# Six modulation units and a shorter routing chain between the output projection and the experts, gate applied at the bank

## The reference, cut to what matters

```python
mod = jax.nn.silu(c) @ w_ada[layer] + b_ada[layer]            # 6 x 1024 columns per layer
sh1, sc1, g1, sh2, sc2, g2 = jnp.split(mod[:, None, :], 6, axis=-1)
hcur = rms_norm(x, norm1_g[layer]) * (1 + sc1) + sh1
...                                                          # layer 0: attention and gMLP, layer 1: conv and stick-breaking
x = x + g1 * mix
hcur = rms_norm(x, norm2_g[layer]) * (1 + sc2) + sh2
x = x + g2 * hierarchical_moe(hcur, ...)
# hierarchical_moe: logits of 4 groups and 4x4 experts; best group, its two best experts
gates = jnp.sum(jax.nn.one_hot(flat_idx, N_EXPERTS) * (g_w * e_w)[..., None], axis=1)
for e in range(N_EXPERTS):                                   # 16 experts, 3 x 2 MB of weights each
    hid = jax.nn.silu(xt @ w_gate[e]) * (xt @ w_up[e])
    y = y + gates[:, e:e + 1] * (hid @ w_down[e])
```

## Time and profile before

| | us |
|---|---|
| median of 3 runs (lowest, highest) | 1408.23 (1408.17, 1416.61) |
| profiled execution, its own time | 1416.04 |
| its span | 1414.4 |
| TensorE busy | 1241.1 (88%) |
| VectorE, ScalarE busy | 355.9, 293.0 |
| mean DMA rate over the span | 248 GB/s |

### The profile page before, as it was taken

One profiled execution on the slowest core, in us unless ns is written; L12 is line 12 of the kernel. 1 busy time (PEld: TensorE's weight loads), 2 busy tenths in 40 slices (PEclk: granted clock), 3 DMA queues, 4 the chain that ended last, 5 costly groups with the idle time before them and its releaser, 6 DMA issues.

```text
span 1414.4 us, 17421 instructions
## 1 busy us (share of the span) xinstructions
PE 1241.1 (88%) x7188; PEld 728.6 (52%) x7191; DVE 355.9 (25%) x1017; ACT 293.0 (21%) x582; POOL 73.4 (5%) x126
## 2 busy tenths in 40 slices
PE   4899995898999969997958799999499999999996
PEld 1656543433334347754434333333286878767772
DVE  0212414211111122852052011111321144333212
ACT  2213302111111121134021111111300345552101
POOL 3000001000000040000000000000000123300000
PEclk8899996999999979999959899999799999999998
DMA  9995972599999997865326899999933433433000
GB/s 344 325 342 200 347 286 62 190 393 395 395 396 394 394 322 282 299 252 178 119 75 251 300 388 395 396 396 394 332 119 133 160 108 124 139 130 130 0 16 30
DMA packets 159061, 351.19 MB, mean 248 GB/s; under 512 B 4852, under 2 KB 7068, under 8 KB 159004
## 3 DMA queue, kind: packets, MB, share of 16 engines
q1 hardware_dynamic: 152776, 340.94, 65.8%
q0 software_dynamic: 4704, 6.50, 1.9%
q10 hardware_dynamic: 1524, 2.95, 0.6%
HBM read 349.25 MB, written 1.12 MB: 248 GB/s over the span
## 4 chain that ended last, share of the span: by engine, by line
PE 66%; DMA 19%; SPq 4%; DVE 4%; ACT 4%; issue 3%; DVEq 0%
PE bank L405 25%; DMA ring<-in_moe_w_up 17%; PE bank L650 13%; PE bank L417 11%; PE bank L439 3%; SPq L357 3%; DMA ring<-in_ev_w_in 2%; PE bank L451 1%; PE bank L671 1%; PE bank L879 1%; PE bank L630 1%; PE bank L460 1%; ACT arena L947 1%; PE bank L471 1%; SPq L322 1%
## 5 line engine op out<-in xcount | busy, mean ns | idle before, releaser
L650 PE MATMUL bank<-ring,arena 128*32 128x512 f32 x3072 | 345.8, 607 | 44.3 <-DMA ring<-in_moe_w_up 20.0
L405 PE MATMUL bank<-arena,ring 128*128 128x256 f32 x1600 | 358.7, 386 | 7.7 <-DVE arena L1311 2.8
L405 PEld LDWEIGHTS bank<-arena,ring 128*128 128x128 f32 x1600 | 306.8, 193 | 59.5 <-issue 11.1
L650 PEld LDWEIGHTS bank<-ring,arena 128*32 128x32 f32 x3072 | 107.1, 112 | 270.8 <-issue 255.5
L417 PE MATMUL bank<-ring,arena 128*128 128x512 f32 x352 | 158.1, 609 | 2.4 <-issue 2.4
L417 PEld LDWEIGHTS bank<-ring,arena 128*128 128x128 f32 x352 | 67.9, 195 | 89.2 <-issue 88.4
L439 PE MATMUL bank<-ring,c_rep 128*32 128x512 f32 x480 | 68.5, 701 | 13.3 <-DMA ring<-in_w_ada 7.5
L1659 DVE TENSOR_TENSOR arena<-arena,bank 128x512 f32<-128x512 f32 x16 | 11.0, 688 | 240.0 <-PE bank L650 240.0
L630 PEld LDWEIGHTS bank<-arena 128*128 128x128 f32 x512 | 60.9, 198 | 12.6 <-issue 11.7
L630 PE MATMUL bank<-arena 128*128 128x128 f32 x512 | 63.4, 284 | 0.0
L671 PE MATMUL bank<-arena 128*128 128x512 f32 x128 | 57.9, 595 | 1.8 <-DVE arena L1667 1.8
(11 more groups left out here) (266 smaller groups left out, 950.8 us busy)
## 6 DMA issues: line engine op xcount, KB each, us to landing
ring<-in_moe_w_gate SPq DMA_DIRECT2D x32, 2048.0 KB, 17.8
ring<-in_moe_w_up SPq DMA_DIRECT2D x32, 2048.0 KB, 19.2
ring<-in_moe_w_down SPq DMA_DIRECT2D x32, 2048.0 KB, 14.4
ring<-in_w_ada SPq DMA_DIRECT2D x24, 2048.0 KB, 12.9
ring<-in_w_in SPq DMA_DIRECT2D x16, 2048.0 KB, 8.8
ring<-in_w_c SPq DMA_DIRECT2D x6, 2048.0 KB, 9.4
ring<-in_ev_w_in SPq DMA_DIRECT2D x5, 2048.0 KB, 20.1
ring<-in_od_w_in SPq DMA_DIRECT2D x5, 2048.0 KB, 9.3
```

Source lines behind the costliest of these rows:

```text
L405: mm = pe.matmul(ps[k0][:, t * S:(t + 1) * S], w[:, k, c:c + P], rhs[:, k, :], start=(k == 0), stop=(k == KT - 1))
L650: mm = pe.matmul(bank[col:col + CHUNK, :], lhs[:, k, col:col + CHUNK], ring[:, s0 + e, cut], start=start, stop=stop, tile_position=(0, col))
```

## The change

1. Order of the units: six `ada` units (17 to 22, 24 to 29) stand right before the experts of each layer; 23 stands before `odo0`.
2. `ada_main` of the six goes to banks 5 to 7 in turn, its partial sums to six places `route_part`, its columns to bank 5; three of the mains run before `turn_x`, three between the logits and the ranks; one `ada_columns` goes before the ranks, five between the ranks and the overflow count. VectorE writes the six sets of columns with one operation (`route_cols`).
3. Logits: eight matmuls with the router's weights stationary, zero-padded to 32 columns, four strips side by side; VectorE copies the bank (`logit_parts`), two matmuls with a selection matrix `sel` sum and turn.
4. The gate's diagonals are made early on ScalarE, in a place of their own (`gate_diag`); its two matmuls lie around those with `sel`.
5. ScalarE loads the tables for the root and for the exponential ahead of their use.
6. The clearing of the banks moves behind `gather(0)`, `late_list` behind the first tokens.
7. `y_pair` is multiplied with the gate as it leaves the bank, both halves on VectorE; after the last pair only four additions are left.
8. `taps` are cut anew, since no columns lie between them: 31 of the first two channel tiles, 19 of the others, and four in each of the heads 0, 1 and 2; the means of the convolution's norm move from the heads 1 and 3 to 3 and 5.

```diff
+    u += [("ada", n) for n in range(17, 23)]
     u += [("moe", 0)] * (6 * PAIRS)
-    for i in range(4):
-        u += [("od", i), ("ada", 17 + 2 * i), ("ada", 18 + 2 * i)]
-    u += [("od", 4)]
-    u += [("ada", n) for n in range(25, 29)]
-    u += [("odo", 0), ("ada", 29), ("odo", 1)]
+    u += [("od", i) for i in range(5)]
+    u += [("ada", 23), ("odo", 0), ("odo", 1)]
+    u += [("ada", n) for n in range(24, 30)]
...
+        ROUTE_UNITS = ((17, 6), (24, 6))
@@ tensor: ada_main
-                if bank is ps[6]:
-                    pe.wait_ge(sem("ada_ready"), n - 1)
-                elif n:
-                    pe.wait_ge(sem("ada_ready"), n)
+                if n:
+                    if bank is ps[4]:
+                        pe.wait_ge(sem("ada_ready"), n)
+                    elif n - 3 >= ROUTE_UNITS[n >= 24][0]:
+                        pe.wait_ge(sem("ada_part_taken"), n - 2)
@@ tensor: experts
-                taken(pe, "gateB" if layer == 0 else "gateD")
                 pe.wait_ge(sem("rw_loaded"), 16 * 7 * (layer + 1))
+                pe.wait_ge(sem("ada_ready"), units_before)
+                for r in range(2):
+                    for g in range(4):
+                        mm = pe.matmul(ps[4][32 * g:32 * g + 32, 0:S], rw[:, 4 * r + g, :], hT[:, 4 * r + g, :],
+                                       start=(r == 0), stop=(r == 1), tile_position=(0, 32 * g))
+                mm.then_inc(sem("logit_parts_full"), 1)
+                gate_row(gate, 0)
+                pe.wait_ge(sem("sel_ready"), layer + 1)
+                pe.wait_ge(sem("logit_parts_taken"), layer + 1)
                 for t in range(TT):
-                    for k in range(KT):
-                        mm = pe.matmul(ps[4][:, 20 * t:20 * t + 20], hT[:, k, t * P:(t + 1) * P], rw[:, k, :],
-                                       start=(k == 0), stop=(k == KT - 1))
+                    mm = pe.matmul(ps[4][:, S + 20 * t:S + 20 * t + 20], logit_parts[:, t * P:(t + 1) * P], sel,
+                                   start=True, stop=True)
                 mm.then_inc(sem("logits_full"), 1)
+                gate_row(gate, 1)
+                for n in range(units - 3):
+                    ada_main()
+                pe.wait_ge(sem("ada_part_taken"), units_before + 4)
+                ada_columns()
                 pe.wait_ge(sem("mask_ready"), layer + 1)
...             # five matmuls of the ranks, now in bank 4
+                for n in range(units - 1):
+                    ada_columns()
                 pe.wait_ge(sem("over_ready"), layer + 1)
...             # overflow count, now in bank 5
                 pe.reg_load(split_reg, split[0:1, layer, 0:1])
                 gather(0)
-                pe.wait_ge(sem("late_ready"), layer + 1)
+                pe.wait_ge(sem("ada_ready"), units_before + units)
+                clear_sums()
                 with pe.Fori(0, PAIRS) as j:
@@ scalar: experts
+                for n in range(3):
+                    ada_part_copy()
                 act.wait_ge(sem("route_max_ready"), 2 * layer + 1)
                 act.activation(rt[:, 40:48], rt[:, 40:48], ACT.Exp).then_inc(sem("route_exp_ready"), 1)
+                gate_row(gate, 0)
+                gate_row(gate, 1)
+                ada_part_copy()
                 act.wait_ge(sem("route_max_ready"), 2 * layer + 2)
                 act.activation(rt[:, 48:50], rt[:, 48:50], ACT.Exp).then_inc(sem("route_exp_ready"), 1)
+                for n in range(ROUTE_UNITS[layer][1] - 4):
+                    ada_part_copy()
...
-                    act.wait_ge(sem("down_full"), j + (done + 1))
-                    act.copy(y_pair[:, 0:512], ps[6][:, :]).then_inc(sem("y_pair_act"), 1)
+            def routed_norm(s, r, n):
+                act.preload_act_table(ACT.Sqrt)
+                act.wait_ge(sem("x_ready"), n)
+                square(s)
+                normalise(s, r)
+                turned(r)
+                act.preload_act_table(ACT.Exp)
@@ vector: experts
+                    dve.wait_ge(sem("down_full"), j + (done + 1))
+                    dve.tensor_tensor(y_pair[:, 0:512], ps[6][:, :], gate_bc[:, 0:512], ALU.mult)
                     dve.wait_ge(unit_done, j * 6 + (first + 6))
-                    dve.tensor_copy(y_pair[:, 512:1024], ps[7][:, :]).then_inc(sem("y_pair_dve"), 1)
+                    dve.tensor_tensor(y_pair[:, 512:1024], ps[7][:, :], gate_bc[:, 512:1024], ALU.mult)\
+                       .then_inc(sem("y_pair_dve"), 1)
                 picks(0)
                 weighted_picks(0)
-                dve.wait_ge(sem("over_full"), layer + 1)
+                left_over(layer)
+                route_cols(layer)
+                tokens_taken(0)
                 late_list(layer)
-                tokens_taken(0)
...
-                for half in range(2):
-                    tmp = (silu_g, hid)
...             # two products and two additions for each half
+                for t in range(TT):
+                    for half in range(2):
                         xv = x[:, t, half * 512:half * 512 + 512]
+                        ins = dve.tensor_tensor(xv, xv, ps[2 * t + half][:, :], ALU.add)
@@ vector: convolution and heads
-            taps(0, 0, 18)
...
+            taps(0, 0, CONV)
             diagonals("gateC")
+            taps(2, 0, 19)
             softplus()
             softplus()
             for h in range(8):
                 if h < 6:
                     softplus()
+                if h < 3:
+                    taps(2, 19 + 4 * h, 23 + 4 * h)
```

More of the change, by code:

```diff
@@ L610, in experts, with clear_sums @@
                   .then_inc(sem("over_full"), 1)
-                pe.wait_ge(sem("zeros_ready"), layer + 1)
-                zero = hidT[:, 0:2, :].rearrange("p a b -> p (a b)").bitcast(BF16)
-                for b in range(4):
-                    mm = pe.matmul(ps[b][:, :], zero[:, 0:P], zero, start=True, stop=True, skip_group_check=True)
+                def clear_sums():
+                    taken(pe, gate)
+                    pe.wait_ge(sem("zeros_ready"), layer + 1)
+                    zero = hidT[:, 0:2, :].rearrange("p a b -> p (a b)").bitcast(BF16)
+                    for b in range(4):
+                        mm = pe.matmul(ps[b][:, :], zero[:, 0:P], zero, start=True, stop=True, skip_group_check=True)
@@ L727, in experts @@
                 scatter(PAIRS - 1)
+                pe.wait_ge(sem("late_ready"), layer + 1)
                 unit[0] = first + 6 * PAIRS
@@ L851, in _ @@
             by_token("odo0", oT)
-            ada_main()
-            ada_columns()
             by_token("odo1", oT)
+            for n in range(3):
+                ada_main()
             turn_x(3)
-            gate_rows("gateD")
             experts(1)
@@ L1049, in gate_rows, with early_diagonals, gate_row @@
                 act.activation(gate_bc[:, 0:512], src[:, :], ACT.Copy, scale=scale).then_inc(free, 1)
+            def early_diagonals(name):
+                n = "ABCDE".index(name[-1])
+                c0 = (16, 40, 64, 88, 112)[n]
+                act.wait_ge(sem("ada_ready"), (6, 12, 18, 24, 30)[n])
+                for k in range(KT):
+                    ins = act.activation(gate_diag[:, k * P:(k + 1) * P], ident, ACT.Copy,
+                                         scale=mod[:, c0 + k:c0 + k + 1])
+                ins.then_inc(sem("diag_ready"), 1)
+            def gate_row(name, b):
+                src, free = full_at(act, name, b)
+                act.copy(gate_bc[:, b * 512:(b + 1) * 512], src[:, :]).then_inc(free, 1)
             def experts(layer):
@@ L1162, in _ @@
             both("od0", aT)
+            both("od1", glT, ACT.Tanh, 0.5)
+            both("od2", qT, scale=0.125)
+            both("od3", kT)
+            tokens("od4", v_tok)
             ada_part_copy()
-            ada_part_copy()
-            both("od1", glT, ACT.Tanh, 0.5)
-            ada_part_copy()
-            ada_part_copy()
-            both("od2", qT, scale=0.125)
-            ada_part_copy()
-            ada_part_copy()
-            both("od3", kT)
-            ada_part_copy()
-            ada_part_copy()
-            tokens("od4", v_tok)
             act.preload_act_table_set("natural_log_exp_and_others")
@@ L1852, in _, with routed_norm @@
             add_mixed(("evo0", "evo1"), (pr[:, 0, :], pr[:, 1, :]))
-            gain(1)
-            normalise(1)
-            diagonals("gateB")
-            turned(1)
-            gate_rows("gateB")
-            taken(dve, "gateB")
+            def routed_norm(s):
+                step(dve.tensor_tensor(sel, ident[:, 0:20], ident[:, 32:52], ALU.add))
+                for g in (2, 3):
+                    step.wait()
+                    ins = dve.tensor_tensor(sel, sel, ident[:, 32 * g:32 * g + 20], ALU.add)
+                    if g == 2:
+                        step(ins)
+                ins.then_inc(sem("sel_ready"), 1)
+                gain(s)
+                normalise(s)
+                turned(s)
```

(1 more changed line is left out.)

161 lines of the change are left out of this document (75 added, 86 removed).

## The result

| | before | after |
|---|---|---|
| median of the runs | 1408.2 us (1405.5 to 1416.61, 4 runs) | 1376.55 us (1374.48 to 1378.22, 4 runs) |
| profiled execution | 1416.04 us | 1374.48 us |
| span in it | 1414.4 us | 1372.8 us |
| mean granted clock of TensorE | 0.935 | 0.951 |

The ratio of the times is 0.9766, with a 95% interval of 0.974 to 0.9792; the medians lie 31.7 us apart. The prediction was 1365 (1354 to 1377), so the measured time lies just inside the upper end of the range.

A forecast was written before the change was run, and what follows sets the result against it. Expert loops were taken as bound by DMA, projections by TensorE, routing by a chain of small steps. Terms -22.0 - 3.6 - 2.9 - 3.2 - 6.2 - 5.3 = -43.2 gave 1372.8 profiled, 1365 median; range 1354 to 1377.

The forecast's parts named there:

- The heads: Layer 1's heads, first scores to end of last head: 46.2 us become 43.3, -2.9, bounds +3 to -6.
- the base for the median: Whole kernel: the median lies 7.8 us under the profiled execution, so 1372.8 for a profiled one becomes 1365.
- The units out of the projections: od0 to od4: twelve units leave, one stays behind od4, -22.0 us; between odo0 and odo1 a further -3.6.
- Rival 2: Heads: late taps or ScalarE's order lengthen them, +3 instead of -2.9, ranks +3 per layer; 1371 to 1377, chance 0.15.
- The chain to the logits: Routing up to the logits, each layer: early table load, gate matmuls off the path, shorter logits; -7.8 us.
- To the ranks: Routing from logits through mask to ranks: VectorE's 6.5 us chain to the mask stays; 0, bounds -1 and +3.
- Behind the ranks: Between ranks and gather: five sets of columns and the overflow matmul take 5.1 us against 3.9, +1.2.
- Gather to first product: Gather to first gate product: clearing +1.2, gather 0.8 shorter, entry stall +3.0 in layer 0, none at layer 1's entry.
- rival 3: Layer 1's loop: its stall gets shorter as the code lies otherwise in its pages; 1357 us, chance 0.13.
- rival 1: Layer 0's first pair: the whole 12.45 us stall falls there, +3 instead of -3.2; 1371 us, chance 0.12.
- The gate at the bank: After the last pair: eight operations become four additions, -2.65 us in each layer, -5.3 in all; nothing late in pairs.
- Rival 4: Expert loops: code no longer stays resident, 14 further pairs lose 10 us each, +140; 1505 us, chance 0.02.

The follow-up runs named there:

- tables late: The changed kernel without the early load of the root's table in the two routing stages; 1377.18 us, one execution.
- fill_start: The changed kernel with thirteen useless matmuls in layer 1's heads and three more ahead of the first turn; 1372.91 us, ratio 0.9714.
- split 2 first: The changed kernel with the code for split 2 put ahead of that for 1 and 3 in the pair loop; 1369.67 us, ratio 0.9689.
- two_gap: The changed kernel with split 2's code first and three useless matmuls ahead of the heads' first turn; 1394.16 us, 1361.39 to 1405.15 in eleven executions.
- two_start: The changed kernel with split 2's code first and all sixteen useless matmuls at and in the heads; 1370.4 us, 1359.89 to 1402.25 in six executions.

## Why the prediction came out as it did

Most terms of the sum were right within 1 or 2 us. The heads failed, by 8.1 us, and the base for the median added 3.6; that the range still holds the measured time is close.

**The units out of the projections** (-22.0): first score 73.0 us behind od0 instead of 96.1, **-23.1**. Chain of after: 256 matmuls of od0 to od3, 32 of od4, then only unit 23.

```profile
509.26 57.52 PE bank L417 x256
566.78 13.73 PE bank L429 x32
580.52 1.90 PE bank L452 x16
```

Between odo0 and the square -5.2 instead of -3.6; the further 1.6 are the clock, 0.90 instead of 0.82 in odo0.

**The heads** (-2.9, with bounds of +3 and -6): measured **+5.2**. This is the step that failed, by 8.1 us. The steps were sized right. From turn to turn the trace of tables late, without fillers, has 4.74 us ahead of the first turn, then 4.75, 6.11, 4.75, 7.52, 5.70, 5.67, 2.95 and 3.44, where the prediction has 4.7, three times 4.9, 7.3, 6.0, 4.3, 2.9 and 3.4; the two that are well over, 6.11 and 5.67, are those with 3.4 us of low clock each. Without these two stretches, I estimate, the heads take 43 us, the predicted 43.3. (The 45.8 of fill_start are at full clock, but with sixteen fillers.) What the term left out is the clock (1.2 GHz where the windows show 0.50, 2.4 where they show 1.00): it has no price for the low one, which held for 23.9 us in after. The same code at 51.4 and 45.6, with 23.9 and 6.8 us of it, shows that: in the long fall TensorE is busy 15.03 of 17.10 us, so slower matmuls lengthen the chain.

The prediction took the removed mains and columns for time that goes; in before they also filled TensorE's waits (40.54 us busy of 46.2, clock 0.96), and without them it is 39.66 of 51.4 at 0.77. Every trace of heads without mains and without all fillers has more low clock (6.8 to 23.9 us) than the two of before (3.4 each), and the two with all fillers have none. How much more is not set by the code alone. Rival 2 had the right direction (+3) with the wrong reason: the taps cost about 2 us, and TensorE waits for them once, as the prediction had it.

**The chain to the logits** (-7.8): counted from the end of the output projection, **-9.5** in layer 0 and -9.2 in layer 1. The clock was at 1.00 instead of 0.70, which the sum took only in part. The table's 1.1 is confirmed alone (1.09). **To the ranks** (0): nothing up to the mask, -0.5 in the ranks. **Behind the ranks** (+1.2): +2.1 in layer 0, five sets of columns 5.90 us; in layer 1 +3.4, since they took 7.1 us, mostly at the low clock, and the gather 5.96 instead of 5.08, which is where its -6.2 became **-4.6**.

**Gather to first product** (+1.2 - 0.8 + 3.0 = +3.4): **+2.9**. The stall added 1.0 (4.26 less 3.23), not 3.0, but the gather got 1.0 longer (5.57 for 4.60) instead of 0.8 shorter, since the clock was low in its first part. A second stall of 1.66 in the first product, not foreseen, brings the two to 5.9, and 0.5 more goes to the low clock in it: restart **-3.0** in layer 0, predicted -3.2. Larger errors cancelled here, and the match is luck in another way too: over the traces the restart lies 48.9 and 50.2 us behind the square in the two of before and 45.9 to 48.5 with after's code (the table's 1.1 taken off), so the term can be read as anything from -0.4 to -4.3. That the stall goes with a jump to code that lies further on was argued from token counts and is now shown by split 2 first: no stall at layer 0's entry, one at layer 1's, both as the order says. A single stall with full queues is 3.4 to 5.0 us, not 12.45; in layer 1 two jumps fall together and more is lost than 4.0 + 4.8. The 12.50 there stayed (12.45 before), so rival 3 fell, as did rival 1.

**The gate at the bank** (-2.65 twice): **-2.76 and -1.93**; alone on before -2.85 and -1.96. That layer 1's is smaller is for the larger part the first trace of before: with the second it is -2.41 in the change and -2.44 alone. For the rest I have no cause.

**Rival 4**, a stall in every pair, did not come in the change, at a chance of 0.02. It did come in part in two_gap, at 5 us in each of five pairs, not at 10 in each of 14.

**The base.** The forecast took the 7.8 us between before's profiled execution and its median off again; after's was 2.1 under its median, so 9.9 us of the sum were never there in the medians. The same-code stages A and E gave 6.3 of them back in this pair of traces. The 11.5 us between 1365 and 1376.55 then come together as 8.1 for the heads, 1.6 and 0.7 for layer 1's restart and loop end, 0.2 for layer 0's restart, less 1.1 and 1.6 for od and odo and 0.1 for layer 0's loop end (7.9), and 9.9 - 6.3 = 3.6 for the base.

**Left open.** Why the clock falls 6 or 9.5 us into the heads, and for how long, with one and the same code; why executions of two_gap and two_start differ by 40 us (that the loop's code is fetched anew is argued from the place and size of the stalls, since nothing in the trace names a fetch); why stage E lasts 402.2 to 402.6 us in some traces and 404.5 to 405.6 in others; why the low clock and the stalls at layer 0's entry have two patterns. None of the experiments puts the units back into the projections, so the -23.1, the largest term, is read from the two chains alone; both traces of before agree on this stretch within 0.2 us, and so do all those of after's code.

## What to carry to other kernels

Work that sits in TensorE's waits may not pay what it seems to when it is taken away: the clock was low for longer in every trace that put nothing in its place, and a shorter queue of work ran between 0.6 us shorter and 5.2 us longer (45.6 to 51.4 us instead of 46.2) from one trace to the next. Such a term needs a second trace before it is believed. Ahead of a loop bound by DMA, count what the first product's end moves, not what the queues carry meanwhile, and put the code of the usual branch first behind the loop's top. When a change of 2 to 3% is taken apart, compare stages with same-code stages beside them and with a second trace of the same kernel; here stage A moved by up to 6.6 us by itself (209.1 to 215.7), and stage B by up to 2.8 in variants of after that leave its code alone.

## What the runs showed of the hardware that was not expected

A single-core program's executions lie 10 us apart (1368.32 to 1378.05) and follow the mean granted clock (0.956 to 0.946); the kernel before does the same (1404.81 at 0.944, 1417.13 at 0.933). Within one stage of the same code the clock is low for 6.8 us in one trace and 23.9 in another. A stall of TensorE at a jump to code further on or back took 2.3 and 3.2 us with idle queues (0 and 5 GB/s in it), and single ones 3.4 to 5.0 with full queues (363 to 408 GB/s). With the other order of the branches and three matmuls in another stage, one trace had such a stall in five of eight pairs, where the same order without them had it in one; executions of one such program differ by over 40 us (1361.39 to 1405.15).
